# Three of six modulation blocks summed on VectorE instead of TensorE, and the MLP gate loaded in the MLP

## The reference

```python
def ada_modulation(cond, w, b):
    m = jax.nn.silu(cond) @ w + b
    return jnp.split(m[..., None, :], N_MOD, axis=-1)

def first_block(...):                      # x: 256 x 2048
    h = rms_norm(x, norm_gain); proj = h @ w_in          # 2048 -> 8192
    y_conv = rms_norm(gated conv of 1024 channels) * silu(z_conv)
    y_attn = rms_norm(causal attention, 8 heads of 128) * silu(z_attn)
    return x + concatenate([y_conv, y_attn]) @ w_out

def second_block(...):
    sh_a, sc_a, g_a, sh_m, sc_m, g_m = ada_modulation(c, w_ada, b_ada)
    csh_a, csc_a, cg_a, csh_m, csc_m, cg_m = ada_modulation(c_ctx, w_ada, b_ada)
    h = modulate(rms_norm_2(x, norm_attn_w), sh_a, sc_a)
    hc = modulate(rms_norm_2(ctx, norm_attn_w), csh_a, csc_a)
    ... q, k, v, u from h; keys and values of the context from hc ...
    x = x + g_a * (concatenate([attn, pool]) @ w_out)
    hm = modulate(rms_norm_2(x, norm_mlp_w), sh_m, sc_m)
    x = x + g_m * (square(relu(hm @ w_up)) @ w_down)     # 2048 -> 8192 -> 2048
    return rms_norm_2(x, final_norm_w)
```

## Time and profile before

| | us |
|---|---|
| median of 3 runs | 1839.15 (1838.42 to 1839.85) |
| the profiled execution | 1841.86 |
| its span | 1840.2 |
| TensorE busy | 1684.9 (92%) |
| VectorE busy | 1023.3 (56%) |
| ScalarE busy | 758.5 (41%) |

### The profile page before, as it was taken

The page is one execution under the profiler, slowest core; times in us unless marked ns, Lnnn a source line. Parts: engine busy times, 40 slices in busy tenths (PEclk is TensorE's granted clock), DMA queues, the critical chain, the costliest instruction groups (busy, mean ns, idle before and its releaser), DMA issues.

```text
span 1840.2 us, 37281 instructions
## 1 busy us (share of the span) xinstructions
PE 1684.9 (92%) x13486; PEld 1566.6 (85%) x13486; DVE 1023.3 (56%) x1504; ACT 758.5 (41%) x1068; POOL 31.5 (2%) x48
## 2 busy tenths in 40 slices
PE   3899999899978977988889869999999999999996
PEld 2788888788877867866779859999999999999996
DVE  5445454455555557556665575544554555455665
ACT  5344444334433334444434435434543454345441
POOL 0000000000000000000000000000000000000000
PEclk9999999899988988999999969999999999999998
DMA  7677777687866773554235525555555555555552
GB/s 307 241 273 258 265 268 262 211 305 289 294 240 218 284 276 134 206 205 173 80 115 172 182 66 183 184 184 177 183 188 180 178 181 187 183 179 181 186 181 89
DMA packets 88372, 374.74 MB, mean 204 GB/s; under 512 B 10256, under 2 KB 10768, under 8 KB 75488
## 3 DMA queue, kind: packets, MB, share of 16 engines
q1 hardware_dynamic: 87120, 369.54, 57.7%
q0 software_dynamic: 1168, 4.00, 0.8%
HBM read 371.40 MB, written 2.10 MB: 203 GB/s over the span
## 4 chain that ended last, share of the span: by engine, by line
issue 73%; PE 13%; DVE 10%; ACT 3%; DVEq 0%; POOL 0%; ACTq 0%; POOLq 0%
DVE lo L1014 3%; PE G L389 3%; PE G L390 3%; PE G L391 3%; ACT hi L691 2%; PE M L594 1%; DVE sm L1308 1%; DVE blk L1014 1%; DVE blk L1321 1%; ACT blk L932 1%; PE ADA L415 1%; PE S L568 1%; PE S L645 0%; DVE blk L1329 0%; DVE resid L1471 0%
## 5 line engine op out<-in xcount | busy, mean ns | idle before, releaser
L1014 DVE TENSOR_TENSOR lo<-raw,hi 128x1024 fp32r<-128x1024 f32 x496 | 607.6, 1225 | 460.4 <-ACT hi L691 426.8
L389 PE MATMUL G<-actA,hi 128*128 128x256 f32 x2368 | 691.3, 292 | 32.4 <-DVE actA L1014 31.9
L691 ACT ACTIVATE hi<-raw 128x1024 fp32r<-128x1024 f32 x496 | 525.0, 1058 | 386.5 <-PE G L391 367.1
L390 PE MATMUL G<-actA,lo 128*128 128x256 f32 x2368 | 676.2, 286 | 0.0
L391 PE MATMUL G<-actA,hi 128*128 128x256 f32 x2368 | 675.6, 285 | 0.0
L389 PEld LDWEIGHTS G<-actA,hi 128*128 128x128 f32 x2368 | 459.9, 194 | 89.9 <-issue 70.4
L390 PEld LDWEIGHTS G<-actA,lo 128*128 128x128 f32 x2368 | 460.9, 195 | 0.3
L391 PEld LDWEIGHTS G<-actA,hi 128*128 128x128 f32 x2368 | 460.5, 194 | 0.0
L389 PE MATMUL G<-actB,hi 128*128 128x256 f32 x1536 | 439.8, 286 | 0.0
L390 PE MATMUL G<-actB,lo 128*128 128x256 f32 x1536 | 437.3, 285 | 0.0
L391 PE MATMUL G<-actB,hi 128*128 128x256 f32 x1536 | 437.2, 285 | 0.0
(11 more groups left out here) (162 smaller groups left out, 883.4 us busy)
## 6 DMA issues: line engine op xcount, KB each, us to landing
raw<-stream_dram SPq DMA_DIRECT2D x496, 512.0 KB, 3.4
ada_raw<-w_ada_dram SPq DMA_DIRECT2D x96, 1024.0 KB, 6.5
x_tok<-x_tok_dram SPq DMA_DIRECT2D x1, 2048.0 KB, 7.9
resid<-xT_dram SPq DMA_DIRECT2D x1, 2048.0 KB, 10.6
ctx_tok<-ctx_tok_dram SPq DMA_DIRECT2D x1, 2048.0 KB, 18.0
W<-ctxT_dram POOLq DMA_DIRECT2D x16, 128.0 KB, 6.3
out_dram<-resid SPq DMA_DIRECT2D x4, 512.0 KB, 2.6
ada_raw<-pool_w_dram POOLq DMA_DIRECT2D x1, 1024.0 KB, 5.1
```

The source lines that it names most:

```text
L389: pe.matmul(bank, hi[:, slot, cols], x[:, k, 0:T], start=(k == 0), stop=False, skip_group_check=True)
L390: pe.matmul(bank, lo[:, slot, cols], x[:, k, 0:T], start=False, stop=False, skip_group_check=True)
L691: return act.activation(dst, src, ACT.Copy)
L1014: return dve.tensor_tensor(dst, a, b, op)
```

## The change

TensorE keeps blocks 0 and 1 (32 row groups, now one in every second unit of the bodies) and block 4 (16, in `w_out` as before). VectorE takes blocks 2 and 3 in the bodies. For a row group it multiplies the four contraction tiles, each 128 x 512, by their columns of `cpad` and adds them (`ada_take`, four instructions); over four row groups the result gathers in `part`, and TensorE then adds only over the 128 partitions (`part_sums`, 4 matmuls of one column), and VectorE adds the bias (`part_add`). Each body has two takes, one after the first split for its unit 1 (in a convolution body after both), one at its very end. The partition sums stand before unit 1 of bodies 2, 4 and 6, behind unit 1 of bodies 8, 10, 12 and 14, and behind unit 1 of `w_out`.

Block 5, the MLP gate, moves from the Q slots to MLP group 0: SP loads one row group every two units, VectorE takes it after every second unit into `part_m`, and behind the group TensorE waits for the last take and adds over the partitions with 16 matmuls of one column.

The turns that are left stand at units 32 and 64 and behind KV unit 2. ScalarE's copy of block 1 moves ahead of the last `high`s before `w_out`, VectorE's bias of block 1 and `scale_a` behind the first split of `w_out`. The loops of VectorE, ScalarE and SP over the bodies are written out.

```diff
+            def ada_take(dst, load):
+                dve.wait_ge(ada_full[1], 16 * load)
+                k = (load - 1) % 4 * 4
+                for m in range(4):
+                    w, c = ada_raw[:, 1, m, :], cpad[:, k + m, 6:7]
+                    if k + m == 0:
+                        seq(dve.tensor_scalar(dst, w, c, None, ALU.mult))
+                    elif m < 3:
+                        seq(dve.scalar_tensor_tensor(dst, w, c, dst, ALU.mult, ALU.add))
+                    else:
+                        dve.scalar_tensor_tensor(dst, w, c, dst, ALU.mult, ALU.add).then_inc(ada_taken, 1)
+                        own(ada_taken)
...
+            def part_sums(n):
+
+                pe.wait_ge(ada_taken, 4 * (n + 1))
+                if n:
+                    pe.wait_ge(part_added, n)
+                for m in range(4):
+                    x = pe.matmul(PART[:, m:m + 1], part[:, m * P:(m + 1) * P], ones[:, 0:1], start=(m == 0), stop=(m == 3),
+                                  skip_group_check=True)
+                x.then_inc(part_summed, 1)
...
             for n in range(UNITS_OUT):
-                unit(At(U_OUT1), n, actB, inB, ada=U_OUT1 + n)
+                unit(At(U_OUT1), n, actB, inB, ada=2 * KT + n)
+                if n == 1:
+                    part_sums(7)
...
             at = At(U_KV)
-            half_unit(at, 0, 0, actC, inC)
-            ada_turn()
-            half_unit(at, 0, 1, actC, inC)
+            unit(at, 0, actC, inC)
             total_sums(1)
             half_unit(at, 1, 0, actC)
             broadcast()
             half_unit(at, 1, 1, actC)
             unit(at, 2, actC)
+            ada_turn()
             unit(at, 3, actC)
...
                 pair_units(7, base + KT + 2, actB)
+                if g == 0:
+                    pe.wait_ge(ada_taken, 3 * KT)
+                    for k in range(KT):
+                        x = pe.matmul(PARTS[:, k:k + 1], part_m[:, k // 4, k % 4 * P:(k % 4 + 1) * P], ones[:, 0:1],
+                                      start=(k == 0), stop=(k == KT - 1), skip_group_check=True)
+                    x.then_inc(part_summed, 1)
...
             for b in range(4):
                 norm_tiles(4 * b, 4, lambda k: col("gain1", k), None)
-            head_body(At(0), False, slice(0, 1))
+            head_body(0)
             dve.wait_ge(act_seq, 4)
             mean_square(ss[:, 2:4], D)
             diagonal(0)
...
                 if g == 0:
+                    for n in range(KT):
+                        up(At(base + n // 2 * 2), n % 2, slice(n, n + 1))
+                        if n % 2 == 1:
+                            ada_take(part_m[:, n // 8], 2 * KT + KT // 2 + n // 2 + 1)
                     dve.wait_ge(acc_zero, 1)
+                    for n in range(KT):
+                        down(At(base + KT + n // 2 * 2), n % 2, slice(n, n + 1), True, None)
+                        if n % 2 == 1:
+                            ada_take(part_m[:, 2 + n // 8], 2 * KT + KT // 2 + KT // 2 + n // 2 + 1)
```

More of the change, by code:

```diff
@@ L132, in program @@
         cpad = sb("cpad", [P, KT, 38])
+        part = sb("part", [P, 512])
         maskb = sb("maskb", [P, 4, P], BF16)
@@ L270, in _, with ada_load @@
             sp.dma_start(ctx_tok[:], t_in["ctx_tok"]).then_inc(ctxtok_in, 16)
+            def ada_load(row, slot, event=None, value=0):
+                if event is not None:
+                    sp.wait_ge(event, value if isinstance(value, int) else sp.snap(value))
+                src = ada_w[row] if isinstance(row, int) else ada_w[bass.ds(sp.snap(row), 1)].rearrange("a p n -> (a p) n")
+                sp.dma_start(ada_raw[:, slot].rearrange("p k n -> p (k n)"), src).then_inc(ada_full[slot], 16)
             for n in range(RING, 2 * RING):
                 weight(n % RING, n)
[L275 to L281, removed]
+            ada_load(0, 0)
+            ada_load(2 * KT, 1)
+            for u in range(U_KV):
+                n = u // 2 + 1
+                if u < U_OUT1 - 2 and u % 2 == 0:
+                    ada_load(n, 0, ada_used, n)
+                elif u < U_OUT1 - 2:
+                    ada_load(2 * KT + n, 1, ada_taken, n)
+                elif u == U_OUT1 - 2:
+                    ada_load(4 * KT, 0, ada_used, 2 * KT)
+                elif u == U_OUT1 - 1:
+                    ada_load(4 * KT + 1, 1, ada_taken, 2 * KT)
+                elif u < U_KV - 2:
+                    e = u - U_OUT1 + 2
+                    ada_load(4 * KT + e, e % 2, ada_used, 2 * KT + e - 1)
+                weight(2 * u % RING, 2 * u + 8)
+                weight((2 * u + 1) % RING, 2 * u + 9)
             with sp.Fori(0, UNITS_KV * 2 // RING) as i:
@@ L284, in _ @@
                     weight(j, i * RING + 2 * U_KV + 8 + j)
[L287 to L301, removed]
-                for j in range(RING):
-                    weight(j, i * RING + 2 * U_POOL + 8 + j)
+            with sp.Fori(0, (2 * U_MLP - 2 * U_Q) // RING) as i:
+                for j in range(RING):
+                    weight(j, i * RING + 2 * U_Q + 8 + j)
+            sp.wait_ge(ada_used, 3 * KT)
+            with sp.Fori(0, KT) as i:
+                ada_load(i + 5 * KT, 1, ada_taken, i + 2 * KT)
+                for j in range(RING):
+                    weight(j, i * RING + 2 * U_MLP + 8 + j)
+            with sp.Fori(0, (2 * UNITS - 2 * U_MLP - 4 * KT - 8) // RING) as i:
+                for j in range(RING):
+                    weight(j, i * RING + 2 * U_MLP + 4 * KT + 8 + j)
             for i in range(4):
@@ L596, in tile_values, with slot @@
                 m.then_inc(head_ready, 1)
-            def slot(at, s, before, last, ada=None):
+            def slot(at, s, before, last):
                 unit(at, s, actA)
@@ L1093, in ada_add, with part_take, part_add @@
                 own(ada_added)
+            def ada_take(dst, load):
[10 more added lines that the diff above has]
+                        own(ada_taken)
+            def part_take(n):
+                if n % 4 == 0 and n:
+                    dve.wait_ge(part_summed, n // 4)
+                ada_take(part[:], n + 1)
+            def part_add(n):
+                dve.wait_ge(part_summed, n + 1)
+                at = 2 * KT + 4 * n
+                tt(adav[:, 0, at:at + 4], PART, col("b_ada", at, 4), ALU.add).then_inc(part_added, 1)
+                own(part_added)
             def head_max():
@@ L1248, in add_squares, with modulation_ready, out_lap @@
                 own(sq_added)
-            def out_lap(at, i, block=None):
+            def modulation_ready():
+                ada_add(1, 1)
+                for r in range(2):
+                    dve.scalar_tensor_tensor(scale_a[:, r], adav[:, r, SC_A:SC_A + KT], 1.0, col("norm_attn", 0, KT), ALU.add,
+                                             ALU.mult).then_inc(scale_ready, 1)
+                    own(scale_ready)
+            def out_lap(at, i, first=False):
                 for j in range(4):
@@ L1254, in out_lap @@
                     split(at, j, 0)
-                    if j == 0 and block is not None:
-                        ada_add(block)
+                    if j == 0 and first:
+                        modulation_ready()
+                    if j == 2 and first:
+                        part_add(7)
                     tt(resid[:, u], resid[:, u], summed(at, j), ALU.add).then_inc(evac_done, 1)
```

146 lines of the change are left out of this document (66 added, 80 removed).

## The result

The changed kernel takes 1861.99 us (median of 4 runs, 1858.61 to 1867.66) against 1839.34 before (4 runs, 1838.42 to 1839.85). The ratio is 1.0123, 95% interval 1.0101 to 1.0145. The forecast was 1848.0 with a range to 1857: the sign was right, the time lies above the range. The profiled execution took 1861.18 (span 1859.1), 19.3 more than that of before. The runs of the changed kernel spread over 9 us, those before over 1.4, and the slower a run, the lower its mean granted clock: 0.951 at 1867.66, 0.955 at 1858.61.

The account below looks back on a forecast made before the run. TensorE was taken to bound the kernel. Bodies -5.0, w_out +1.5, KV -3.7, Q slots +3.6 and MLP +12.5 sum to +8.9: 1850.8 against the profiled run, 1848.0 against the median, range 1832 to 1857.

Parts of the forecast that it names:

- the wait at the MLP boundary: Between MLP groups 0 and 1, TensorE waits 5.4 us for VectorE's last take; part of the boundary's +12.5.
- KV: At KV's start, without the turn that waited for ScalarE's copy, the sums end earlier: -3.7 us.
- The Q slots: First pair of row groups -2.0 us; six inner slots gain nothing, four dip in clock at 1.4 each: together +3.6.
- the price of a stall: In bodies, TensorE waits for its row group: 0.9 us in a head body, 2.8 in a convolution body.
- its feedback: In convolution bodies a stall makes raw tiles, hi, lo and takes later: +1.35 us from the second on.
- Bodies 2 to 7: Bodies with two fewer row groups and stalls or partition sums: -7.0 us in all.
- The sums at the boundary: 32 one-column records between MLP groups 0 and 1: 2.9 us at full clock, up to 7.5, taken as 5.0.
- before w_out: The last take stands before VectorE's diagonal; with body 15's lateness, +3.7 us for everything behind on VectorE.
- The offset: Whole run: the median before lies 2.7 us below the profiled run, so 1850.8 became 1848.0.
- the row lands in time: Rival in the bodies: TensorE's row lands within 7.1 us of the load before it, no body stalls; 1828, chance 0.17.
- The loaded queue: Rival in the bodies: the load series takes 0.7 us longer, 12 bodies stall so much more; +8, 1856, chance 0.11.
- the two on the Q slots: Rivals in the inner Q slots: no clock dip, 1842.4, chance 0.12; all six slots dip, 1850.8, chance 0.05.

Follow-up runs that it names:

- the combined version: Changed kernel with row group and raw tiles ahead of SP's wait, gate back in the Q slots, three VectorE edits: 1804.42 us, ratio 0.9811 to before.
- experiment 1: Changed kernel with SP's load for a take placed behind the two raw tiles and TensorE's next row group: 1831.89 us, ratio 0.9957 to before.
- experiment 2: Changed kernel with the MLP gate's wait and 16 one-column matmuls moved behind unit 2 of MLP group 1: 1855.94 us, ratio 1.0088 to before.
- experiment 6: Changed kernel with the gate's 16 one-column matmuls in four pieces behind units 2, 4, 6, 8 of MLP group 1: 1851.44 us, ratio 1.0068 to before.

## Why the prediction was wrong

**Right.** A take lasts 2.33 + 0.75 = 3.1 us (forecast 3.1, by 1.27 ns a column; a 512-column instruction took 752 ns on average). The take's end, the landing and the length of the stall in body 11 are each within 0.3. So is the wait at the MLP boundary, and KV gave 3.2 of 3.7. The Q slots behaved as forecast: the pair had filled a wait, its removal gave nothing, and half clock followed in four of the six, at 0.5 to 1.3 us each instead of 1.4.

**The step that failed: the price of a stall.** The forecast priced each stall of the bodies at its length and the lateness it hands on. It knew the restart at half clock, and charged it at the MLP boundary and in the Q slots, but in the bodies it put it at nothing. Four of the five dips lie in bodies 10 to 14, where 5.8 is missing. From TensorE's row group to the next S these bodies take 11.56, 11.61, 11.60, 11.47 and 10.10, in sum 56.3 where the forecast has 5 x 10.3 = 51.5: that is 4.8 of the 5.8. The other 1.0 is when the row group starts: at S + 20.5 in bodies 10 and 13, and at S + 18.5 in 11, 12 and 14, where the forecast, with its feedback, has 19.1 on average (its body lengths less 10.3). Bodies 2 to 7 kept the sign of their forecast: three of them had no stall, two had 0.9, and only body 5, with 1.85, had a dip.

**A wait that was not seen.** The bias of block 0 (`ada_add`) stands on VectorE behind the take at the end of body 7, and TensorE's first row group of block 1 waits for it: 2.87 in body 8, where the forecast had -1.2 and the trace +1.4. The prediction asked what stands behind a take on VectorE for the diagonals, and not here; the combined version moved the bias ahead of the take, and body 8 was 1.5 shorter than before.

**Sizes.** The sums at the boundary ran wholly at half clock, 6.9 instead of 5.0, and before w_out the wait grew by 5.1 instead of 3.7. A body that drops two row groups and does not stall is 2.4 shorter, not 2.0 (experiment 1), which is part of why bodies 0, 1 and 9 came out better than forecast. Before w_out the last splits were late too: ScalarE's timeline in the changed kernel has `hi` waiting for a raw tile that stood behind SP's wait:

```profile
539.26 1.06 ACT L711 ACTIVATE hi<-raw 128x1024 fp32r<-128x1024 f32 x1 [3.56 <-DMA raw<-stream_dram]
```

**The offset.** The forecast subtracted the 2.7 us by which the profiled execution before lay above its median. The profiled execution after lay 0.8 *below* its median. That is 3.5 of the 14 us between forecast and result, and none of it is in the stages, whose 10.5 would have put the time above the range by themselves (1848.0 + 10.5 = 1858.5).

**The rivals.** The first, that the row lands in time, did not come: the four loads of a series landed in order of issue in the changed kernel too. On this the Trainium skill's sentence ("DMA: Bandwidth & Descriptors", "Queues, rings and completion order") that completion is "not FIFO per issuing engine" was not seen at work on one queue. The loaded queue came in part: from the first issue of the series to the landing of the row group it was 9.9 to 10.0 in bodies 11, 12, 14 and 15, as in the earlier trace rows, but 11.3 and 11.5 in bodies 10 and 13. Of the two on the Q slots neither came, since four of six dipped. On the restarts the Trainium skill ("TensorE: Matmul & The Clock Gate", section "HAM oscillation — how this bites in real kernels") describes the very pattern, a wait for a DMA, then matmuls at half rate, each time anew. The trace agrees in part: five waits of 1.8 to 4.5 us have a dip of 3.4 us behind them, and five others, of 0.9 to 3.4 us, have none.

## What to carry to other kernels

A wait in the program of the engine that issues DMAs holds back everything behind it: put ahead of it every load that another engine needs soon, above all those that an in-order engine consumes. Work taken from the bottleneck engine pays only where that engine had no wait beside it (the row groups of the inner Q slots were free), and a new wait costs its length and, where the clock falls with it, 1.4 to 1.5 us more here. When work moves to a second engine, list what stands behind it there, the small instructions too.

## What the runs showed of the hardware

- 32 one-column matmul records in one stretch of 4.5 us, with no wait before or in it, dropped the granted clock from 1.00 to 0.50 for what followed; the same records in four pieces of 8 with 96 matmuls between them did not (experiments 2 and 6).
- Waits did not decide alone. Waits of 1.85, 2.53, 2.69, 1.84 and 4.50 us had a dip behind them in the changed kernel; those of 2.87 in body 8, 1.75 in body 14 and 3.36 in body 15 had none. The same wait of 2.87 in body 8 did have one in experiments 1 and 2 (mean clock 0.58 and 0.52 in the 3.4 us behind it).
- One queue carried 331 GB/s over a whole body (experiment 1) when its issuing engine did not stand.
